# Expert blocks of 64 rows as two column tiles in a hybrid decoder step

## What is computed

```python
def hier_moe(h, lw):
    g_sel = argmax(t @ router_wg + router_bg)
    top_v, top_i = top_k(e_logits[rows, g_sel], 2)
    w_sel = softmax(top_v) * g_prob[rows, g_sel]
    gates = einsum('tk,tke->te', w_sel, one_hot(idx, 32))
    hg = einsum('td,edf->tef', t, lw['w_gate'])
    hu = einsum('td,edf->tef', t, lw['w_up'])
    a = silu(hg) * hu * gates
    y = einsum('tef,efd->td', a, lw['w_down'])
```

## Time and profile before

| | |
|---|---|
| median of 3 runs | 1962.01 us |
| span of the profiled execution | 1958.0 us |
| its mean granted clock of TensorE | 0.908 |
| PE busy | 1731.6 us (88%) |
| DVE, ACT, POOL busy | 607.9, 511.3, 199.3 us |
| moved by DMA | 356.11 MB, mean 182 GB/s |
| chain that ended last | PE 79%, DVE 11% |

### The profile page before, as it was taken

How to read it: one execution, slowest core, us unless ns; L and a number is a source line. 1 busy time by engine, 2 the same in 40 slices (tenths; PEclk the granted TensorE clock), 3 DMA queues, 4 the chain that set the end, 5 groups by cost and what they waited for, 6 DMA issues and landing times.

```text
span 1958.0 us, 24553 instructions
## 1 busy us (share of the span) xinstructions
PE 1731.6 (88%) x7098; PEld 1153.6 (59%) x7099; DVE 607.9 (31%) x1528; ACT 511.3 (26%) x1023; POOL 199.3 (10%) x362
## 2 busy tenths in 40 slices
PE   6989898979779999999499898988895999999992
PEld 4766454444557777777367654445445777777771
DVE  3454773111421111111335458620124111111114
ACT  3331243131112222222214222421310222222222
POOL 0003300000011111111200041000000111111112
PEclk9989989679679999999789898995995999999996
DMA  5232204310639999997521012123215699979965
GB/s 204 73 118 98 71 1 130 108 51 39 227 126 345 345 345 344 344 346 270 182 92 51 22 50 65 48 82 107 75 61 191 229 347 343 347 281 344 346 249 177
DMA packets 207234, 356.11 MB, mean 182 GB/s; under 512 B 9506, under 2 KB 157314, under 8 KB 206786
## 3 DMA queue, kind: packets, MB, share of 16 engines
q1 hardware_dynamic: 181842, 263.18, 40.1%
q0 software_dynamic: 14160, 50.69, 7.0%
q10 hardware_dynamic: 11168, 41.42, 5.2%
HBM read 305.36 MB, written 49.90 MB: 181 GB/s over the span
## 4 chain that ended last, share of the span: by engine, by line
PE 79%; DVE 11%; issue 3%; ACT 3%; DMA 3%; SPq 1%; POOL 0%; DVEq 0%; POOLq 0%; ACTq 0%
PE bank L1800 23%; PE bank L1815 12%; PE bank L1487 11%; PE bank L1738 7%; PE bank L1631 2%; PE bank L1630 2%; PE bank L1685 2%; PE bank L1674 2%; PE bank L1654 2%; PE bank L1673 2%; PE bank L1780 2%; PE bank L1509 2%; PE bank L1751 2%; PE bank L1806 1%; DVE rb L1422 1%
## 5 line engine op out<-in xcount | busy, mean ns | idle before, releaser
L1800 PE MATMUL bank<-rg,rb 128*128 128x256 f32 x1056 | 238.9, 386 | 1.7 <-DVE rb L1411 1.7
L1800 PEld LDWEIGHTS bank<-rg,rb 128*128 128x128 f32 x1056 | 204.7, 194 | 44.2 <-issue 14.8
L1487 PE MATMUL bank<-ra,rb 128*128 128x288 f32 (+1 forms) x896 | 225.5, 415 | 3.7 <-DVE ra L954 3.7
L1800 PE MATMUL bank<-re,rb 128*128 128x256 f32 x1024 | 226.2, 379 | 0.0
L1800 PEld LDWEIGHTS bank<-re,rb 128*128 128x128 f32 x1024 | 194.9, 190 | 39.8 <-issue 15.3
L1487 PEld LDWEIGHTS bank<-ra,rb 128*128 128x128 f32 (+1 forms) x896 | 171.4, 192 | 55.2 <-issue 4.3
L1422 DVE TENSOR_TENSOR rb<-rb,bank 128x256 f32<-128x256 f32 x65 | 27.4, 421 | 410.3 <-PE bank L1800 410.3
L905 ACT ACT_TABLE_LOAD x65 | 83.4, 1283 | 219.3 <-issue 219.3
L1815 PE MATMUL bank<-rg,rb 128*128 128x512 f32 x264 | 122.0, 605 | 3.5
L1815 PE MATMUL bank<-re,rb 128*128 128x512 f32 x256 | 118.3, 605 | 3.3
L1426 DVE COPY ra<-bank 128x512 f32<-128x512 f32 x65 | 45.0, 692 | 208.1 <-PE bank L1815 208.1
(11 more groups left out here) (348 smaller groups left out, 2219.8 us busy)
## 6 DMA issues: line engine op xcount, KB each, us to landing
y_rows<-ra ACTq DMA_DIRECT2D x65, 512.0 KB, 7.6
rg<-in_w_gate SPq DMA_DIRECT2D x32, 1024.0 KB, 7.7
rg<-in_w_up SPq DMA_DIRECT2D x32, 1024.0 KB, 10.7
rg<-in_w_down SPq DMA_DIRECT2D x32, 1024.0 KB, 12.6
re<-in_w_gate SPq DMA_DIRECT2D x32, 1024.0 KB, 7.8
re<-in_w_up SPq DMA_DIRECT2D x32, 1024.0 KB, 10.6
re<-in_w_down SPq DMA_DIRECT2D x32, 1024.0 KB, 12.4
rg<-in_cache SPq DMA_DIRECT2D x128, 192.0 KB, 3.7
```

The lines of the kernel that those rows point to most:

```text
L1487: ins = mm(bk[:mrows, 0:HALF], win[:, n % 4, k, :mrows], hT[:, k, cols], start=k == 0, stop=k == KT - 1)
L1800: ins = mm(bank[2 + half][:, 0:DE], xT[:, k, :], wgu[s][:, k, half * DE:(half + 1) * DE], start=k == 0, stop=k == KT - 1)
```

## The change

A block has 64 rows (`B`), so an expert has one block and another one for each further 64 rows. The matmuls of a block are split in two that write partitions 0 to 63 and 64 to 127 of one bank: for gate and up each half has 128 of the gate columns and the same 128 of the up columns, for down each half has 512 of the 1024 columns. Gate and up now come out together. DVE alone copies the transposed rows (one bank), ACT alone copies the result (one bank), and the store is two transfers of 64 rows x 2 KB. The wait for the next block's rows moves ahead of the last pair of gate and up products. The table for Silu is loaded ahead of the loop. The tables of the router have 60 instead of 46 columns, the steps that count blocks run to nine instead of five, and those that find a row's place in its block run behind the sum over experts. The weights are loaded by the same transfers into the same places; only the view has one more dimension.

```diff
+B = 64
+SPILL = T // B
+MAXBLK = EXPERTS + 2 * T // B
+TABLE = MAXBLK + SPILL + 1
...
-        xg = cut(ra, 0, D)
-        ysb = cut(ra, 1024, D)
+        xg = cut(ra, 0, D)[0:B, :]
+        ysb = cut(ra, 1024, 512)
...
-        wgu = [cut(r, at, KT, 512) for r, at in slot_at]
+        wgu = [cut(r, at, KT, 2, 2 * P) for r, at in slot_at]
...
-                        xg, None, h_rows, bass.IndirectOffsetOnAxis(ap=slot_now[:, 0:1], axis=0)) \
+                        xg, None, h_rows, bass.IndirectOffsetOnAxis(ap=slot_now[0:B, 0:1], axis=0)) \
...
+                nc.scalar.preload_act_table(ACT.Silu)
...
-                        act.wait_ge(S["gate_done"], ever + c + 1)
-                        fn(act1, bank[2][:, 0:DE], ACT.Silu).then_inc(S["silu_done"], 1)
+                        act.wait_ge(S["gu_done"], ever + c + 1)
+                        fn(act1, bank[2][:, 0:P], ACT.Silu).then_inc(S["silu_done"], 1)
                         act.wait_ge(S["at_done"], ever + c + 1)
-                        copy(actT, bank[4][:, 0:DE].rearrange("p (k n) -> p k n", k=2)).then_inc(S["actt_ready"], 1)
-                        rows_transposed(ever + c + L + 2)
+                        copy(actT, bank[4][:, 0:P].rearrange("p (k n) -> p k n", k=2)).then_inc(S["actt_ready"], 1)
                         act.wait_ge(S["down_done"], ever + c + 1)
-                        act.wait_ge(S["y_stored"], (ever + c + 1) * 16)
-                        copy(ysb[:, 0:512], bank[5][:, :]).then_inc(S["y_act"], 1)
+                        act.wait_ge(S["y_stored"], (ever + c) * 32 + 16)
+                        copy(ysb, bank[5][:, :]).then_inc(S["y_act"], 1)
                         act.wait_ge(S["y_act"], ever + c + L + 2)
-                        act.wait_ge(S["y_vec"], ever + c + L + 2)
-                        act.dma_start(y_rows[bass.ds((first + c) * P, P), :], ysb).then_inc(S["y_stored"], 16)
+                        for n in range(2):
+                            act.dma_start(y_rows[bass.ds((first + c) * B, B), 512 * n:512 * n + 512],
+                                          ysb[64 * n:64 * n + 64, :]).then_inc(S["y_stored"], 16)
...
-                for k in (2, 3, 4):
-                    link(V.scalar_tensor_tensor(r_nb, r_cnt, float(k * P), r_nb, ALU.is_gt, ALU.add))
+                for k in range(2, SPILL):
+                    link(V.scalar_tensor_tensor(r_nb, r_cnt, float(k * B), r_nb, ALU.is_gt, ALU.add))
...
-                        V.tensor_tensor(act2, act1, bank[3][:, 0:DE], ALU.mult).then_inc(S["act_ready"], 1)
+                        V.tensor_tensor(act2, act1, bank[2][:, P:2 * P], ALU.mult).then_inc(S["act_ready"], 1)
...
-                            for half, signal in ((0, "gate_done"), (1, "gu_done")):
-                                for k in range(KT):
-                                    ins = mm(bank[2 + half][:, 0:DE], xT[:, k, :],
-                                             wgu[s][:, k, half * DE:(half + 1) * DE], start=k == 0, stop=k == KT - 1)
-                                ins.then_inc(S[signal], 1)
-                            rows_transpose(ever + c + L + 2, 0)
+                            for k in range(KT):
+                                if k == KT - 1:
+                                    pe.wait_ge(S["gathered"], (ever + c + L + 2) * 16)
+                                for h in range(2):
+                                    ins = mm(bank[2][64 * h:64 * h + 64, 0:DE], xT[:, k, :], wgu[s][:, k, :, h * P:(h + 1) * P],
+                                             start=k == 0, stop=k == KT - 1)
+                            ins.then_inc(S["gu_done"], 1)
+                            rows_transpose(0)
                             pe.wait_ge(S["act_ready"], ever + c + 1)
-                            for k in range(2):
-                                ins = tr(bank[4][:, k * P:(k + 1) * P], act2[:, k * P:(k + 1) * P], ident)
-                            ins.then_inc(S["at_done"], 1)
-                            rows_transpose(ever + c + L + 2, 1)
+                            tr(bank[4][:, 0:P], act2, ident).then_inc(S["at_done"], 1)
+                            rows_transpose(1)
...
-                            for n in range(2):
-                                for k in range(2):
-                                    ins = mm(bank[5 + n][:, :], actT[:, k, :], wdn[s][:, k, 512 * n:512 * n + 512],
-                                             start=k == 0, stop=k == 1)
+                            for k in range(2):
+                                for n in range(2):
+                                    ins = mm(bank[5][64 * n:64 * n + 64, :], actT[:, k, :],
+                                             wdn[s][:, k, 512 * n:512 * n + 512], start=k == 0, stop=k == 1)
                             ins.then_inc(S["down_done"], 1)
```

More of the change, by code:

```diff
@@ L361, in hybrid_step @@
         r_diff = cut(rb, 505, TT, GROUPS + 1)
-        r_any, r_rank, r_hi = (cut(rb, 530 + 160 * k, TT, EXPERTS) for k in range(3))
-        r_h2, r_l2 = (cut(rb, 1010 + 10 * k, 2 * TT) for k in range(2))
+        r_any, r_rank = (cut(rb, 530 + 160 * k, TT, EXPERTS) for k in range(2))
+        r_h2, r_l2, r_hi = (cut(rb, 1010 + 10 * k, 2 * TT) for k in range(3))
         r_nb = cut(rb, 1062, EXPERTS)
@@ L609, in gather @@
                 def gather(block):
[L610 removed]
+                    nc.gpsimd.tensor_copy(slot_now[0:B, :], slots[0:B, block]).then_inc(S["slot_copied"], 1)
                 def gather_rows(n):
@@ L625, in _ @@
                 with pool.Fori(0, EXPERTS) as e:
-                    count = pool.value_load(blocks[0:1, bass.ds(e, 1)], min_val=1, max_val=TT)
+                    count = pool.value_load(blocks[0:1, bass.ds(e, 1)], min_val=1, max_val=SPILL)
                     first = pool.value_load(blocks[0:1, bass.ds(e + 33, 1)], min_val=0, max_val=MAXBLK)
@@ L890, in _ @@
                 act.wait_ge(S["route_ready"], L + 1)
+                nc.scalar.preload_act_table(ACT.Silu)
                 copy(sm[:, 200:201], sm[:, 190:191]).then_inc(S["y_act"], 1)
[L893 to L898, removed]
                 with act.Fori(0, EXPERTS) as e:
-                    count = act.value_load(blocks[0:1, bass.ds(e, 1)], min_val=1, max_val=TT)
+                    count = act.value_load(blocks[0:1, bass.ds(e, 1)], min_val=1, max_val=SPILL)
                     first = act.value_load(blocks[0:1, bass.ds(e + 33, 1)], min_val=0, max_val=MAXBLK)
@@ L1376, in _ @@
                 V.tensor_copy(blocks[0:1, 0:99], r_tab[0:1, 0:99]).then_inc(S["route_ready"], 1)
[L1377 to L1382, removed]
+                starts = r_tab[:, 33:65].unsqueeze(1).to_broadcast([P, TT, EXPERTS])
+                for src, dst in ((r_rank, r_l2), (starts, r_h2)):
                     for k in range(2):
@@ L1416, in _ @@
                 with dve.Fori(0, EXPERTS) as e:
-                    count = dve.value_load(blocks[0:1, bass.ds(e, 1)], min_val=1, max_val=TT)
+                    count = dve.value_load(blocks[0:1, bass.ds(e, 1)], min_val=1, max_val=SPILL)
                     ever = dve.value_load(blocks[0:1, bass.ds(e + 66, 1)], min_val=0, max_val=DEPTH * MAXBLK)
@@ L1773, in _, with rows_transpose @@
                 pe.wait_ge(S["route_ready"], L + 1)
-                def rows_transpose(n, half):
-                    if half == 0:
-                        pe.wait_ge(S["gathered"], n * 16)
-                    for k in range(4):
-                        at = (4 * half + k) * P
-                        ins = tr(bank[half][:, k * P:(k + 1) * P], xg[:, at:at + P], ident)
+                def rows_transpose(half):
+                    for k in range(4 * half, 4 * half + 4):
+                        ins = tr(bank[0][:, k * B:(k + 1) * B], xg[:, k * P:(k + 1) * P], ident[0:B, 0:B])
                     if half == 1:
@@ L1784, in _ @@
                 before = pe.value_load(blocks[0:1, 66:67], min_val=0, max_val=DEPTH * MAXBLK)
-                rows_transpose(before + L + 1, 0)
-                rows_transpose(before + L + 1, 1)
+                pe.wait_ge(S["gathered"], (before + L + 1) * 16)
+                mm(bank[0][:, 0:B], xg[:, 0:P], ident[0:B, 0:B], start=True, stop=True)
+                rows_transpose(0)
+                rows_transpose(1)
                 with pe.Fori(0, EXPERTS // RING) as g:
                     for s in range(RING):
-                        count = pe.value_load(blocks[0:1, bass.ds(g * RING + s, 1)], min_val=1, max_val=TT)
+                        count = pe.value_load(blocks[0:1, bass.ds(g * RING + s, 1)], min_val=1, max_val=SPILL)
                         ever = pe.value_load(blocks[0:1, bass.ds(g * RING + (66 + s), 1)], min_val=0,
```

57 lines of the change are left out of this document (27 added, 30 removed).

## The result

The changed kernel took 1895.28 us (median of 4 runs, 1888.7 to 1901.11) against 1962.41 for the kernel before on the same chip: 0.9659 of it, 95% interval 0.9642 to 0.9675. It is faster, by 67 us where 131 were forecast, and the time lies above the range of 1797 to 1885. The profiled execution took 1898.75 us with a span of 1897.0, 69.7 above the forecast span of 1827.3. All readings of after are from it.

What follows compares the result with a forecast made beforehand. PE sets the pace before (12.17 us a block), DMA after (10.92 for an expert with one block). Span 1958.0 - 64.3 (layer 0) - 68.0 (layer 1) + 1.6 (routing) = 1827.3, with 4.0 more 1831 us; range 1797 to 1885.

Steps and rivals of the forecast that it cites:

- the gather's loop: Row-list copy, issue, landing, last gate and up pair, hand-over and transposes until buffer release: 9.5 us, below DMA's 10.92.
- a lag of 17 us: Layer 1, experts 16 to 22: 12 blocks at 9.5 us fall behind DMA, 17 us left at the end; 4 taken.
- The DMA as next bound: In the expert loops, weights 9.42 us per expert plus store and gather 1.50 per block: 10.92 us, longer than PE's 7.5.
- The halves: Products on PE's two column halves run side by side: gate and up 3.41 us, down 1.71 per block.
- PE's block: Gate and up 3.41, hand-over 2.4 and down 1.71: 7.5 us per block, 8.8 with the table load.
- the table load: Silu's activation table, 1.28 us in each block before, goes ahead of the loop and leaves the block.
- the first loads: First weight load inside each layer's loop issues 5.1 us earlier, at 567.0 and 1529.7 us.
- A loop outlasts the DMA: Rival, 0.06: the store's loop behind 1 MiB of weights takes 11.8 us a block, 2009 us, slower.
- The gather gets no cheaper: Rival, 0.18: the gather costs 1.34 us instead of 0.80 for 69 blocks, +37, 1868 us.
- the deciding 11.14: Time per block, 791/71 us, above which the 71 blocks make the new kernel slower than the old.
- The clock falls: Rival counted within the range: PE waits some 3.4 us per block; at half clock its block is 10.3 us, below 10.92.
- No overlap: Rival, 0.03: the halves of PE's products don't run side by side, 12.65 us a block, +107, 2069 us.

Runs made afterwards that it cites:

- sixth_weights: Changed kernel, with the loop loading one sixth of each expert's weights after the four experts loaded ahead; 1751.03 us, ratio 0.8923 to the kernel before.
- half_rows: Changed kernel, with the loop's gather bringing 2 KB of each row instead of 4; 1823.36 us unprofiled, not compared; layer 0 steps 9.60 us.
- fixed_rows: Changed kernel, with the loop's gathers landing in a buffer nobody reads and PE not waiting for them; 1809.12 us, ratio 0.9227 to the kernel before.
- sixth_one_store: As sixth_weights, with each block's store issued as one transfer of 128 pieces of 2 KB; 1701.57 us, ratio 0.8676 to the kernel before.
- busy_wait: Changed kernel, with two unread 128 x 512 multiplies on PE ahead of the gather wait; 1900.2 us, ratio 0.9693 to the kernel before.
- late_list: Changed kernel, with PE's row wait moved behind the product's transpose and the row list copied before the buffer wait; 1839.28 us, 0.938 of the kernel before.

## Why the prediction was wrong, point by point

**Where the 70 us are.** Layer 0, from the first load of the loop to the end of the last down products: forecast 567.0 to 884.7, 317.7 us; measured 565.45 to 911.42 (the last eight start at 909.48 and take 1.94), 346.0. Layer 1: forecast 1529.7 to 1855.9, 326.2; measured 1489.87 to 1861.85, 372.0. That is 28 and 46 us too much. The rest of the span came out some 4 us shorter, so the miss of 69.7 lies in the loops.

**The failed step is the gather's loop.** Its sum was 0.76 + 6.1 + 0.43 + 2.2 = 9.5 us, or 8.8 with a transfer that shrinks with the rows. The pieces 0.76 and, together, 2.63 (2.40 measured) were right. The landing was not: 6.1 us of before was taken as an upper end, and it came out at 7.3. Before, the issue at 703.00 and 6.1 us of landing end at 709.1, and the next block's down products, ahead of which the rows are transposed, start at 714.19: nobody waited for the landing. A duration that was hidden was carried over as if only its bytes made it. sixth_weights and half_rows part it: 4.2 us without most of the weights, 6.4 with half the bytes. The changed kernel shows it without any edit, too. Behind the second blocks of layer 0, which load nothing, two gathers went out while the engines were nearly idle (a share of 0.23 from 615 to 620 us, 0.15 from 675 to 680), at 616.31 and at 677.42. They landed in 3.7 and 4.0 us, and the turns in which they flew took 9.27 and 9.41 us instead of some 10.5. The Trainium skill, "DMA: Bandwidth & Descriptors", section "Anatomy of one DMA — SWDGE (gpsimd) path", gives a transfer about 2 us and its bytes over 436 GB/s, which for these 262 KB would be an estimate of 2.6 us. All the landings of 64 rows measured here are above it, 3.7 us with nearly idle engines and 7.3 in the full queue, nearly three times the estimate, so for a queue that other transfers fill the trace does not agree.

**The comparison was with the wrong number, too.** The loop of 9.5 was set against 10.92, the DMA's price of an expert with one block. But an expert's second block loads nothing and still takes a turn of the loop: over the layer the DMA asks 313.3/33 = 9.5 us a block in layer 0 and 317.8/36 = 8.8 in layer 1. Measured turns of 10.49 and 10.34 are above both, so it was the loop that ended last, even below 10.92. The prediction saw this for layer 1, as a lag of 17 us with a loop of 9.5, and took 4 in the hope of a shorter landing. With 9.5 the loop gives 36 x 9.5 = 342 us for layer 1 between its multiplies, already 16 over the forecast 326; the other 30 of the measured 372 are 36 times the excess of 0.84. In layer 0 a loop of 9.5 would have given 314 us, within the forecast, so by this sum its 28 us come from the landing.

**The DMA as next bound: right, behind the loop.** With the wait gone fixed_rows took 310 us for layer 0 and waited for weights. After reads a share of 1.06 to 1.08 between 700 and 860 us, and would look bound by DMA from this alone; that PE waits for the gather there, and that the share is 0.67 and 0.76 in other stretches and 0.81 to 0.92 in the four stretches of 50 us from 1650 to 1850, tells otherwise.

**The halves, PE's block, the table load: right.** 28 passes in 3.37 us; 7.5 us for PE's block, met by sixth_one_store at 7.52; no table load. The routing and the first loads came out within 3 us. The weights moved at 323 GB/s (68.47 MB in 84.7% of 250 us), not faster than before.

**The rivals.** *A loop outlasts the DMA* is what happened, through the gather, where the prediction thought of the store (6.4 us to landing now, 7.7 before); it wasn't slower than before because 10.4 lies under the deciding 11.14. *The gather gets no cheaper*: 0.94 us on the engines, between the forecast 0.80 and 1.34. Half the packets at the old price would be 0.67 on any number of engines; in the packet records one of 4 KB took 234 ns (median) now and 162 before. The most packets of one gather under way at once were 13 to 18 from 600 to 850 us, 16 to 19 before; in the two gathers on nearly idle engines, 17 and 15 that took 0.17 us or less each. This speaks against a gather that is left on half of the engines, but no record names the engine of a packet, so it isn't excluded. The Trainium skill, "DMA: Bandwidth & Descriptors", section "The descriptor swizzle", gives partitions 0 to 63 to engines 0 to 7 in a transfer to 128 partitions; for these 64 no run here shows it. The time of 1868 was passed by another mechanism. *The clock falls*: it did, to 0.83, at no cost in this kernel, as the prediction had bounded. *No overlap*: excluded.

Not tried: a second buffer for the gathered rows, which would take the landing out of the turn altogether.

## What to carry to other kernels

When an engine gets faster, add up every loop that passes through one single buffer (release, issue, landing, use, release) and compare it with the mean price of the other bounds over the whole loop, not with the price of the typical turn. A landing read from a queue that is hidden today is no price of its bytes: measure it at the load that it will have, and take it as a lower end if the load rises. Short of a second buffer, ask for the data as late in the turn as the code allows and give the buffer back as early: here that, with the list copied ahead, gave 56 us more in a few lines. Then read the turn again: the next bound was the engine that stores the result and starts the next block.

## What the runs showed of the hardware

A gather of half as many rows landed later than the whole one: 7.3 against 6.1 us, with the weights' queue at 84.7% of the engines against 77.8% before. In the packet records the first packet starts 2.4 us after the issue before and 3.8 after (medians; between 2.7 and 4.3 after), but 1.6 in the two gathers on nearly idle engines and in those of sixth_weights. So the added delay lies ahead of the data; what holds it there stays open.

Two small transfers issued from ACT one behind the other took 1.15 to 1.17 us of its queue, one took 0.34, and a turn of 8.28 us shrank to 7.52 when the two were made one.

A clock at half speed in a whole group of products (3.52 us against 1.94 for the eight down passes) cost nothing in the changed kernel, since these lay under the gather's flight: busy_wait raised the clock of the stretch from 0.83 to 0.97, and layer 0 took 345.1 us instead of 346.2. In late_list, where the gather no longer holds the turn, turns with the slow products took 10.0 us and those with the fast ones 8.4 (medians).
